# A second attention pass on one Trainium2 core: value products by two key blocks, row scores of two heads in two row halves, a pair of heads ahead

## The reference, cut to what matters

```python
def attend(q, k, v):                      # 16 query heads, 4 key heads, width 64
    q = q.reshape(bsz, lq, A_NKV, A_REP, A_HEADDIM)
    s = jnp.einsum('bqgrd,bkgd->bgrqk', q, k).astype(F32) * (A_HEADDIM ** -0.5)
    p = jax.nn.softmax(s, axis=-1).astype(v.dtype)
    o = jnp.einsum('bgrqk,bkgd->bqgrd', p, v)
    ...
    q = rmsnorm(q.reshape(bsz, L, A_NH, A_HEADDIM), q_norm)   # attn_mixer
    k = rmsnorm(k.reshape(bsz, L, A_NKV, A_HEADDIM), k_norm)
    ql = apply_rope(ql, cos, sin)
    kl = apply_rope(kl, cos, sin)
    k_all = jnp.concatenate([kc, kl], axis=1)
    v_all = jnp.concatenate([vc, vl], axis=1)
    ...
    o_lat = (ol * jax.nn.silu(gl)) @ out_w
```

## Time and profile before

| | us |
|---|---|
| median of 3 runs (2494.2 to 2494.78) | 2494.69 |
| the profiled execution, its own time | 2490.51 |
| span of its trace | 2488.4 |
| attention, first `key_scores` to first output tile | 148.1 (2281.49 to 2429.58) |
| one pair in the middle (2338.01 to 2356.33) | 18.3 |

### The profile page before, as it was taken

How to read it: one execution, slowest core, us unless ns; L and a number is a source line. 1 busy time by engine, 2 the same in 40 slices (tenths; PEclk the granted TensorE clock), 3 DMA queues, 4 the chain that set the end, 5 groups by cost and what they waited for, 6 DMA issues and landing times.

```text
span 2488.4 us, 33109 instructions
## 1 busy us (share of the span) xinstructions
PE 2375.7 (95%) x12118; PEld 1934.2 (78%) x12118; DVE 1446.3 (58%) x1768; ACT 778.2 (31%) x1632; POOL 1393.0 (56%) x1236
## 2 busy tenths in 40 slices
PE   8989999999998899999998999999999997998998
PEld 6767877888777687788876898998998995875446
DVE  7984311224677541111357797888788798327763
ACT  3353110102332520110135434334333333423651
POOL 8736766678777276666774343443443441453455
PEclk9999999999998999999998999999999999998999
DMA  4211344323222034422232110110110112120001
GB/s 166 88 51 63 141 169 152 110 85 110 85 85 93 18 119 165 168 108 102 90 120 102 51 51 34 51 51 34 51 51 34 51 51 79 51 85 34 1 1 68
DMA packets 32142, 200.09 MB, mean 80 GB/s; under 512 B 4144, under 2 KB 8240, under 8 KB 9136
## 3 DMA queue, kind: packets, MB, share of 16 engines
q1 hardware_dynamic: 24560, 159.87, 18.0%
q10 hardware_dynamic: 7488, 38.87, 4.5%
HBM read 192.44 MB, written 5.24 MB: 79 GB/s over the span
## 4 chain that ended last, share of the span: by engine, by line
PE 75%; DVE 16%; issue 4%; ACT 3%; POOL 1%; DMA 0%; DVEq 0%; SPq 0%; ACTq 0%; POOLq 0%
PE ps L444 37%; PE ps L747 13%; PE ps L989 4%; DVE convd L2252 3%; PE ps L1099 2%; PE ps L843 1%; PE ps L1086 1%; PE ps L865 1%; DVE convd L2266 1%; PE ps L471 1%; PE ps L882 1%; PE ps L646 1%; PE ps L852 1%; PE ps L1087 1%; PE ps L854 1%
## 5 line engine op out<-in xcount | busy, mean ns | idle before, releaser
L366 POOL TENSOR_SCALAR whi<-wraw 128x512 fp32r<-128x512 f32 x568 | 388.0, 711 | 965.2 <-PE ps L747 437.9
L370 POOL TENSOR_TENSOR wlo<-wraw,whi 128x512 fp32r<-128x512 f32 x568 | 862.7, 1549 | 0.0
L444 PE MATMUL ps<-uhi,whi 128*128 128x512 f32 x896 | 354.9, 396 | 15.7 <-POOL wlo L352 11.2
L444 PE MATMUL ps<-uhi,wlo 128*128 128x512 f32 x896 | 350.0, 391 | 0.0
L444 PE MATMUL ps<-ulo,whi 128*128 128x512 f32 x896 | 349.7, 390 | 0.0
L747 PE MATMUL ps<-inhi,whi 128*128 128x384 f32 (+1 forms) x784 | 243.5, 345 | 5.8 <-DVE inlo L2196 4.6
L747 PE MATMUL ps<-inlo,whi 128*128 128x384 f32 (+1 forms) x784 | 236.7, 337 | 0.0
L747 PE MATMUL ps<-inhi,wlo 128*128 128x384 f32 (+1 forms) x784 | 236.6, 336 | 0.0
L2085 DVE TENSOR_TENSOR h<-h,ps 128x1024 f32<-128x1024 f32 x40 | 48.8, 1221 | 307.1 <-PE ps L444 307.1
L444 PEld LDWEIGHTS ps<-uhi,whi 128*128 128x128 f32 x896 | 168.8, 188 | 58.8 <-POOL wlo L352 11.2
L444 PE MATMUL ps<-hidhi,whi 128*128 128x512 f32 x512 | 201.0, 393 | 0.0
(11 more groups left out here) (456 smaller groups left out, 4703.0 us busy)
## 6 DMA issues: line engine op xcount, KB each, us to landing
wraw<-in_wstream SPq DMA_DIRECT2D x150, 1024.0 KB, 4.8
modraw<-in_modw ACTq DMA_DIRECT2D x24, 1024.0 KB, 4.8
hspill<-hres ACTq DMA_DIRECT2D x1, 3072.0 KB, 9.1
hback<-hspill ACTq DMA_DIRECT2D x1, 3072.0 KB, 10.0
h<-in_x ACTq DMA_DIRECT2D x2, 1024.0 KB, 5.1
gw<-in_gates ACTq DMA_DIRECT2D x2, 512.0 KB, 3.4
pT<-in_pT ACTq DMA_DIRECT2D x2, 512.0 KB, 4.5
proj<-proj ACTq DMA_DIRECT2D x16, 64.0 KB
```

What stands on the lines that cost most here:

```text
L366: pool.tensor_scalar(whi[:, s, c], wraw[:, s, c], 1.0, 0.0, ALU.mult, ALU.add).then_inc(wraw_read, 1)
L370: ins = pool.tensor_tensor(wlo[:, s, c], wraw[:, s, c], whi[:, s, c].bitcast(F32), ALU.subtract)
L444: mm = pe.matmul(ps[:, 2 * bank + m, :], a[:, w, c:c + P], b[:, kb, :], start=(n == 0 and i == 0), stop=(n == KB - 1 and i == 2))
```

## The change

It touches the opening and the pairs, on all five engines.

- **Row scores.** A unit is now 128 queries of *both* heads of a pair: head e uses 64 rows of the array (its channels against the key's high part, in `K2` for e = 0 and `K1` for e = 1), four matmuls a unit, 32 units. A unit fills all four banks 4 to 7, so a unit waits for the maximum of the unit before. One `maximum` reduces both heads (32 in all), one `turn_max` and one `max_rows` serve a pair (two matmuls; 4x1024). They run up to two pairs ahead, four units a pair (five in pairs 0 to 2, one in pair 6, none in pair 7), at places given by a table.
- **Values.** `attend(b, i)` takes two key blocks, i = 0 to 2.
- **Sums.** POOL adds all six blocks in pairs 0 to 6, so `prob_sums` has half its matmuls there; in pair 7 it is as before.
- **Copies.** `Q1` of pairs 2 to 7 comes from one rounded ACT copy of the pair (`row_q`, `qrow`) through four transfers of 128 KB by SP; the rests of pairs 1 to 7 are computed by POOL (`qrest`) and copied into `QL` by two transfers. SP issues these after the weight tiles up to T_ATT + 12, the last two tiles after them. PE waits for them at a pair's start.
- **Opening.** `head_sums_q(4)` and the `rope_turn`s stand inside the gate tiles; ACT takes all logarithms and exponentials before the first tanh; four units of row scores stand inside the fourth gate tile.
- `recips` and `o_hi` of pair b come one pair later on ACT.

In the diff below the parts are, in this order: the table of places, SP, POOL, `row_scores`, the loop over a pair on PE, and `maximum`.

```diff
+ROW_SLOTS = {0: ("0K", "0E", "1V", "2K", "2E"), 1: ("0K", "0E", "1K", "2K", "2E"), 2: ("0V", "0E", "1V", "2K", "2E")}
+EVEN_SLOTS = ("0E", "1V", "2K", "2E")
...
+        for b in range(1, PAIRS):
+            p = b % 2
+            sp.wait_ge(q_hi, b + 1)
+            if b >= 2:
+                sp.wait_ge(sT_ps, 2 * NC * (b - 1))
+                for e in range(2):
+                    for half in range(2):
+                        sp.dma_start(Q1[p][64 * half:64 * half + 64, e, :].bitcast(F32),
+                                     qrow[64 * e:64 * e + 64, b, :].bitcast(F32)).then_inc(land[p], 16)
+            sp.wait_ge(q_lo, b)
+            for e in range(2):
+                sp.dma_start(QL[p][0:64, e, :].bitcast(F32), qrest[64 * e:64 * e + 64, b, :].bitcast(F32)).then_inc(land[p], 16)
...
-            for kb in range(1, 5):
+            for kb in range(1, NC if b + 1 < PAIRS else NC - 1):
...
+                if kb == 3 and b + 2 < PAIRS:
+                    pool.wait_ge(q_hi, b + 3)
+                    pool.tensor_tensor(qrest[:, b + 2, :], qb_[:, b + 2, :], qrow[:, b + 2, :].bitcast(F32), ALU.subtract
+                                       ).then_inc(q_lo, 1)
...
-            if u >= 2:
-                pe.wait_ge(mx_r, u - 1)
+            if r:
+                pe.wait_ge(mx_r, r)
...
-            q = Q1[b % 2][e][:, t * P:(t + 1) * P]
-            o = u % 2 * 1024
-            pe.matmul(ROWS[:, o:o + S], q, K1[j % 2][:, 0:S], start=True, stop=True)
-            pe.matmul(ROWS[:, o + S:o + T], q, K1[j % 2][:, S:T], start=True, stop=True).then_inc(s_ps, 1)
+            for n, (k0, k1) in enumerate(((0, S), (S, T))):
+                for e in range(2):
+                    h = slice(64 * e, 64 * e + 64)
+                    q = Q1[b][h, e, t * P:(t + 1) * P] if b < 2 else qrow[h, b, t * P:(t + 1) * P]
+                    mm = pe.matmul(ps[:, 4 + 2 * e + n, 0:k1 - k0], q, (K1 if e else K2)[j % 2][h, k0:k1],
+                                   start=True, stop=True)
+            mm.then_inc(s_ps, 1)
...
+            for i in range(3):
+                key_scores(b, 2 * i)
+                slot(b, f"{i}K")
+                if b or i:
+                    attend(b - (i == 0), (i - 1) % 3)
+                if i == 2 and b:
                     prob_sums(b - 1)
+                slot(b, f"{i}V")
+                key_scores(b, 2 * i + 1)
+                slot(b, f"{i}E")
+                if b + 1 < PAIRS and i == (1 if b else 2):
+                    turn_max(b + 1)
...
+            V.tensor_reduce(nm[:, r // 4, :, r % 4], ps[:, 4:8, :].rearrange("p (e a) n -> p e (a n)", e=2)[:, :, 0:T],
+                            AX.X, ALU.max, negate=True).then_inc(mx_r, 1)
```

More of the change, by code:

```diff
@@ L973, in _, with lat_tile @@
             v_chunk(c)
-        def lat_tile(k, unit, src, t0, read, kwait=None):
+        def lat_tile(k, unit, src, t0, read, kwait=None, inside=None):
             hi, lo = src
@@ L2660, in _ @@
-        gate(3)
-        rope_add(8)
-        rope_add(9)
-        dve.wait_ge(rp_r, 10)
-        maximum(4)
-        maximum(5)
-        maximum(6)
-        max_rows(0)
+        for n in range(6, 10):
+            rope(n)
+        k_split(0)
+        V.memset(QL[0][64:128, :, :].bitcast(F32), 0.0)
+        q_split()
+        maximum(0)
+        gate(2)
+        maximum(1)
+        dve.wait_ge(rp_r, 10)
+        clear_k(1)
+        maximum(2)
+        maximum(3)
+        max_rows(0)
+        gate(3)
@@ L2668, in _ @@
+        for r in range(4, 7):
+            maximum(r)
+        k_split(1)
         maximum(7)
-        clear_k(1)
         max_rows(1)
-        for b in range(PAIRS):
-            more = b + 1 < PAIRS
-            if b:
-                gated(b - 1)
-            if more:
-                q_split(2 * b + 2)
-                maximum(8 * b + 8)
-                maximum(8 * b + 9)
-                q_split(2 * b + 3)
-                maximum(8 * b + 10)
-                maximum(8 * b + 11)
-            if b:
-                normed(b - 1)
-            if more:
-                maximum(8 * b + 12)
-                maximum(8 * b + 13)
-                if b % 2 == 0 and b // 2 + 1 < KVH:
-                    k_split(b // 2 + 1)
-                max_rows(2 * b + 2)
-                maximum(8 * b + 14)
-                maximum(8 * b + 15)
-            if b:
-                o_lo(b - 1)
-            if more:
-                max_rows(2 * b + 3)
+        maximum(8)
@@ new lines, in _ @@
+        maximum(9)
+        gated(0)
+        maximum(10)
+        maximum(11)
+        max_rows(2)
+        maximum(12)
+        maximum(13)
+        gated(1)
+        maximum(14)
+        maximum(15)
+        k_split(2)
+        maximum(16)
+        normed(0)
+        max_rows(3)
+        maximum(17)
+        maximum(18)
+        for b in range(3, PAIRS):
+            gated(b - 1)
+            if b + 1 < PAIRS:
+                maximum(4 * b + 7)
+            o_lo(b - 3)
+            if b % 2 == 0 and b // 2 + 1 < KVH:
+                k_split(b // 2 + 1)
+            if b + 2 < PAIRS:
+                maximum(4 * b + 8)
+            normed(b - 2)
+            if b + 1 < PAIRS:
+                max_rows(b + 1)
+            if b + 2 < PAIRS:
+                maximum(4 * b + 9)
+                maximum(4 * b + 10)
@@ L2696, in _ @@
+        o_lo(PAIRS - 3)
+        normed(PAIRS - 2)
         gated(PAIRS - 1)
+        o_lo(PAIRS - 2)
         normed(PAIRS - 1)
```

318 lines of the change are left out of this document (153 added, 165 removed).

## The result

The changed kernel took 2467.12 us (median of 4 runs, 2465.04 to 2469.72) beside 2494.44 for the kernel before: a ratio of 0.9892, with a 95% interval from 0.9874 to 0.9909. The prediction was 2469.7 with a range from 2462 to 2481. The profiled execution took 2469.72 by its own time, the slowest of the four.

A forecast was written before the change was run, and what follows sets the result against it. PE's own instructions bound the pairs, idle time and slow clock the opening; 10.8 + 148.1 - 133.1 = 25.8, less 0.8 for ports, is 25.0 off 2490.51: 2465.5, or 2469.7 as median (4.2 above); range 2462 to 2481.

The forecast's parts named there:

- The opening: Ahead of the last attention's first key score: PE's idle times and slow clock mostly go, so it starts 10.8 us earlier.
- the turn's wait: End of the opening: the turn of the maxima on PE waits 0.6 us for DVE's fourth maximum.
- the slow stretch: End of the opening: 3.0 us of PE work at half clock returns to full clock, gaining about 1.5 us.
- rival (d): Pairs 0 to 2: short waits drop the clock to 0.50, costing 13 us a pair; three such pairs give 2509; chance 0.03.
- Pairs 0 to 7: The last attention's pairs: 133.1 us in all against 148.1, middle pairs at 15.9, pair 1 longer at 19.3.
- Pair 7: The last pair: no row units or turn, but its own values, sums and 1.2 of waits; 17.8 us against 18.25.
- Row units: Row scores in the pairs: two row halves overlap, so a unit takes 0.63 us: 0.10 + 0.33 + 0.20.
- Rival (a): Row scores: the row halves don't overlap, a unit takes 1.0, 10.4 us less gain, 2480; chance 0.12.
- Values and sums: PE in a pair: a value group takes 1.97 us; values gain 0.8 and sums 0.9 of 2.4 us a pair.
- Other engines: In a pair: POOL is busy 13.0 us, DVE 12 to 13, ACT about 10; none reaches 15.9.
- The 0.8 us for ports: Taken off the summed gain of 25.8 us because two-input DVE operations are longer beside POOL's additions.
- Copies: Six transfers of 128 KB a pair land in 9 us at most, within the 15.9 of a pair, and cost nothing.

The follow-up runs named there:

- a4_rows_behind_gate: The changed kernel with the four row units of pair 0 behind the fourth gate tile instead of inside it: 2479.6 us, ratio 0.9952 to the kernel before.
- a10_units_twice: The changed kernel with each row unit in the pairs issuing its four matmuls twice: 2477.7 us, ratio 0.9938 to the kernel before.

## Why the prediction was right

- **The opening.** 10.8 forecast, 10.8 measured (73.97 less 63.18). Windows of it, the kernel before and then the changed one:

```profile
2207.52:2281.49 73.97, 64.94 (x249) 45.42 (x247) 49.81 (x57) 24.30 (x21) 32.98 (x32) 0.96 0.16 57
```

```profile
2212.07:2275.25 63.18, 62.89 (x249) 43.63 (x247) 50.01 (x49) 22.85 (x22) 34.52 (x33) 1.00 0.19 67
```

PE's idle time fell from 9.0 to 0.3 us and its busy time by 2.1: the two parts of the forecast, 8.8 of idle time less the turn's wait, and 1.5 and 0.4 for the slow stretch and the row units. The turn's wait was 0.29 for 0.6. The claim that a high clock follows from waits of 1.2 us or less held in the changed kernel, but `a4_rows_behind_gate` shows how near rival (d)'s mechanism was: waits of 1.86 and 2.31 us were enough. Its price there was 3.6 us, not the 13 a pair that the rival put on it, since the clock came back within the first pair.
- **Pairs 0 to 7.** Forecast 16.1, 19.3, 17.7, three times 15.9, 14.5, 17.8; measured 16.06, 19.34, 17.36, 15.92, 15.95, 15.96, 14.76, 18.43. The sum is 133.8 for 133.1. The longer pair 1 is there, with the waits that the prediction named: 0.88 for the maximum row, 0.83 and 0.73 for maxima. Pair 7 is the largest miss, 0.6, and its sign is wrong: 17.8 was to be a gain on the 18.25 of before, and 18.43 is a loss. The forecast had 1.2 us of waits there and named none of them; there are two of 0.30 ahead of key scores and the 0.80 of the last value group, which needs both blocks' exponentials. Counted from start to start these three cost 1.8.
- **Row units.** 0.64 for 0.63. The parts were off against each other by little: 0.35 of streaming and 0.29 for the changes of tiling, where the prediction had 0.33 and 0.30. Rival (a) falls by `a10_units_twice`.
- **Values and sums.** A group 1.97 with its entry, as forecast. The 0.9 for the sums is 0.85. The 0.8 for the values was right as a difference of two kernels, but of it only 0.5 comes back when blocks are split again, since in the new order some second blocks have a row unit or the turn behind them, which then needs no entry. The runs put back 0.85 (sums), 0.5 (values) and 0.2 (row halves) of the 2.4 us a pair; the other 0.8, with the turn and the vanished wait in it, is read from rows alone.
- **Other engines.** POOL 13.0 to 14.6 and DVE 11.0 to 12.3 in a middle pair for 13 and 12 to 13. The 0.8 us for ports was not needed: PE waited in no middle pair. `normed` was stretched all the same, to 2.87 in the longest:

```profile
2383.70 2.87 DVE L2669 TENSOR_TENSOR qb<-qb,gs 128x512 f32<-128x512 f32 x1
```

- **Copies.** On time with some 10 us to spare; twice as many cost nothing.
- **The number.** 25.0 us were forecast and 25.1 lie in opening and section together. That these meet to 0.1 is luck in part: the terms gave 25.8, the pairs came out 0.7 longer than their terms, most of it in pair 7, and the 0.8 taken off for ports, which cost nothing, made up for it. The profiled execution took 2469.72, not 2465.5, for the 4.55 us ahead of the attention. The median came out at 2467.12 for 2469.7; that it is met to 2.6 is within what the executions differ by.
